# Norm sums taken beside the output products, first products begun behind each tile, values with high and low part in one stationary tile

## What is computed

```
for l in range(DEPTH):
    sh1, sc1, ga1, sh2, sc2, ga2 = split(silu(c) @ w_mod[l] + b_mod[l])      # one set for latents, one for context
    u = rmsnorm(h, g_pre_mix[l]) * (1 + sc1) + sh1
    y = token_mixers(u)         # four branches of 8 heads, gates, w_branch, w_out
    h = h + ga1 * rmsnorm(y, g_post_mix[l])
    u = rmsnorm(h, g_pre_ffn[l]) * (1 + sc2) + sh2
    a, b = split(u @ w_ffn_in[l])
    h = h + ga2 * rmsnorm((silu(a) * b) @ w_ffn_out[l], g_post_ffn[l])
```

## Time and profile before

| | |
|---|---|
| median of 3 runs | 2121.2 us (2120.85 to 2124.73) |
| the profiled execution's time | 2117.97 us |
| its span | 2116.2 us |
| TensorE busy | 1899.1 us, 90% of the span |
| VectorE, ScalarE, GpSimd busy | 1182.9, 865.7, 644.3 us |
| mean granted TensorE clock | 0.938 |

### The profile page before, as it was taken

The page is one execution under the profiler, slowest core; times in us unless marked ns, Lnnn a source line. Parts: engine busy times, 40 slices in busy tenths (PEclk is TensorE's granted clock), DMA queues, the critical chain, the costliest instruction groups (busy, mean ns, idle before and its releaser), DMA issues. The chain is left out here.

```text
span 2116.2 us, 32133 instructions
## 1 busy us (share of the span) xinstructions
PE 1899.1 (90%) x10899; PEld 1637.3 (77%) x10899; DVE 1182.9 (56%) x2360; ACT 865.7 (41%) x1870; POOL 644.3 (30%) x611
## 2 busy tenths in 40 slices
PE   8778899999988899968999999869999999979998
PEld 7566677777777777756777888757788888879997
DVE  6246666666556645268777522346564446645653
ACT  2245444444433443331222232246555545444453
POOL 6333343445444443020000100134435544311100
PEclk9989999999999999968999999779999999979998
DMA  7112333333332223215566433112344433435663
GB/s 280 53 49 60 82 85 96 95 90 108 88 84 65 70 57 122 72 60 154 174 187 193 128 95 97 45 37 64 81 120 101 115 81 91 115 95 164 183 183 109
DMA packets 391788, 223.69 MB, mean 106 GB/s; under 512 B 53398, under 2 KB 387532, under 8 KB 390604
## 3 DMA queue, kind: packets, MB, share of 16 engines
q1 hardware_dynamic: 389324, 218.50, 36.6%
q10 hardware_dynamic: 2304, 3.15, 0.5%
HBM read 218.44 MB, written 3.15 MB: 105 GB/s over the span
## 5 line engine op out<-in xcount | busy, mean ns | idle before, releaser
L1605 PE MATMUL bank<-Uhi,w_ring 128*128 128x512 f32 (+2 forms) x1664 | 604.7, 363 | 42.7 <-issue 27.1
L1606 PE MATMUL bank<-Ulo,w_ring 128*128 128x512 f32 (+2 forms) x1664 | 588.5, 354 | 0.0
L1607 PE MATMUL bank<-Uhi,w_ring 128*128 128x512 f32 (+2 forms) x1664 | 588.0, 353 | 0.0
L1361 DVE TENSOR_TENSOR w_ring<-load_ring,w_ring 128x512 fp32r<-128x512 f32 (+1 forms) x432 | 301.4, 722 | 260.1 <-ACT w_ring L1194 244.8
L1194 ACT ACTIVATE w_ring<-load_ring 128x512 fp32r<-128x512 f32 (+3 forms) x640 | 369.1, 603 | 85.2 <-PE bank L1607 74.6
L1605 PEld LDWEIGHTS bank<-Uhi,w_ring 128*128 128x128 f32 (+1 forms) x1664 | 327.1, 197 | 90.1 <-issue 32.3
L1154 POOL TENSOR_TENSOR w_ring<-load_ring,w_ring 128x512 fp32r<-128x512 f32 (+2 forms) x208 | 249.1, 1201 | 375.4 <-ACT w_ring L1194 237.7
L1607 PEld LDWEIGHTS bank<-Uhi,w_ring 128*128 128x128 f32 (+1 forms) x1664 | 326.3, 196 | 42.6
L1606 PEld LDWEIGHTS bank<-Ulo,w_ring 128*128 128x128 f32 (+1 forms) x1664 | 327.6, 197 | 36.6
L1605 PE MATMUL bank<-Z,w_ring 128*128 128x512 f32 (+2 forms) x784 | 275.6, 352 | 11.8 <-DVE Z L1500 6.1
L1606 PE MATMUL bank<-Z,w_ring 128*128 128x512 f32 (+2 forms) x784 | 269.5, 344 | 0.0
(11 more groups left out here) (114 smaller groups left out, 2414.0 us busy)
## 6 DMA issues: line engine op xcount, KB each, us to landing
load_ring<-in_w_in SPq DMA_DIRECT2D x204, 256.0 KB, 3.0
load_ring<-in_w_ffn_in SPq DMA_DIRECT2D x176, 256.0 KB, 3.2
Y<-in_w_mod SPq DMA_DIRECT2D x96, 256.0 KB, 2.8
load_ring<-in_w_ffn_out SPq DMA_DIRECT2D x80, 256.0 KB, 3.1
mod_place<-in_w_mod SPq DMA_DIRECT2D x64, 256.0 KB, 2.8
load_ring<-in_w_branch SPq DMA_DIRECT2D x64, 256.0 KB, 2.9
mod_w<-in_w_mod SPq DMA_DIRECT2D x8, 1024.0 KB, 13.8
load_ring<-in_w_in SPq DMA_DIRECT2D x64, 128.0 KB, 2.6
```

The source lines that it names most:

```text
L1361: dve.tensor_tensor(w_ring[:, slot, 1, 0:sz], load_ring[:, plan.slot['load', key], 0:sz], w_ring[:, slot, 0, 0:sz].bitcast(F32), ALU.subtr ...
L1605: pe.matmul(dst, lhs[0], rhs[0], start=start, stop=False)
L1606: pe.matmul(dst, lhs[0], rhs[1], start=False, stop=False)
L1607: return pe.matmul(dst, lhs[1], rhs[0], start=False, stop=stop)
```

## The change

1. **Sums beside the outputs.** `yev` evacuates y already multiplied by its gate coefficient (one instruction per side). Instead of `sq` and `sqmm` three quantities are made for each tile: y squared (`ysq`, ScalarE from PSUM), z squared (`zsq`, ScalarE, z the scaled y), H times z (`hz`, VectorE). GpSimd adds tiles 1 to 6 into three sums (`yadd`, `zadd`, `hadd`). At the end step `sums` has TensorE reduce the three sums and the three last tiles, 24 one-column products at 512 tokens.
2. **Turnover.** The next norm's sum is worked out from these: sum(h^2) + 2 r sum(h z) + r^2 sum(z^2) (`moment`, five small VectorE operations, and a power on GpSimd, `pow`). `bccopy` copies the first broadcast from PSUM to SBUF. `post` works in place on Y, tiles 2, 5 and 7 on GpSimd, the others on VectorE, and is interleaved with `apply`.
3. **Products behind each tile.** The first four projections (ckv, cq 0, cq 1, kr; or fa and fb of f = 0 and 1) form a group with four accumulators: `gmm` kt does their twelve products for one kt as soon as `ap_lo` of that kt is there, with weights loaded as one row piece of 416 or 512 columns. Their evacuations and the latents' norms follow behind the whole group.
4. **Values.** V is stored with high and low part side by side, 128 columns per head. `pv` takes two passes per key tile instead of three. `ov` becomes: ScalarE copies the lower half of the result to SBUF (`o_raw`), VectorE adds the upper half, ScalarE writes the high part, VectorE the low part.
5. **Modulation and splits.** In layer 1's modulation a `modw` costs its number of sides and a `modsum` 0.5, the rate is 3.7, and f = 0 and 1 have no calls. Low parts of layer 0's fa and fb pieces go to GpSimd. The coefficients of the next layer are formed ahead of w_ffn_out.

```diff
+MOD_RATE_FFN = 3.7
+POST_POOL = (2, 5, 7)
...
-        while self.todo and self.todo[0][1][0] == self.layer and self.owed >= 1:
+        while self.todo and self.todo[0][1][0] == self.layer:
             kind, key, j = self.todo[0]
+            l, ch = key
+            sides = 2 if l == 0 or ch < 16 else 1
+            cost = 1 if l == 0 else sides if kind == 'modw' else 0.5
+            if self.owed < cost:
+                break
...
+    def apply(nm, l, which, n, first, posts=None):
...
         for kt in range(KT + 1):
             if kt < KT:
                 p.take('tmp', ('ap', nm, kt), ('ap_hi', (nm, kt)), ('ap_full', (nm, kt)))
                 p.take('fil', ('ap', nm, kt), ('ap_lo', (nm, kt)))
                 p.step('apA', (nm, kt), l=l, which=which, n=n)
+                for step in posts.get(kt, ()):
+                    step()
             if kt:
                 p.step('apB', (nm, kt - 1), n=n)
+                p.step('gmm', (first, kt - 1))
...
+    def turnover(nmo, nm, l, which, n, first):
...
+        p.step('sums', nmo, n=n, what=('ysq', 'hz', 'zsq'))
+        p.step('mstat', nmo, nh=1, dim=D, n=n, after=('sums_done', nmo))
+        p.step('wide', nmo, n=n, of=1)
+        p.take('bc', ('bc', nmo), ('bc_copied', nmo))
+        p.step('bcast', nmo, n=n)
+        p.step('bccopy', nmo, n=n)
+        p.step('moment', nm, n=n)
+        p.step('pow', nm, n=n)
+        post(nmo, 0, n)
+        post(nmo, 2, n)
+        p.step('wide', nm, n=n, of=4)
+        p.take('bc', ('bc', nm), ('ap_scaled', (nm, KT - 1)))
+        p.step('bcast', nm, n=n)
+        later = {0: (1,), 1: (3, 5), 2: (4,), 3: (6, 7)}
+        apply(nm, l, which, n, first, {i: [(lambda kt=kt: post(nmo, kt, n)) for kt in kts] for i, kts in later.items()})
...
-        if key[0][0] not in ('gate', 'up', 'y', 'fa', 'fb') or key[0][0] == 'gate' and key[0][1][0] == 0:
+        what = key[0][0]
+        if what not in ('gate', 'up', 'y', 'fa', 'fb', 'first') or what in ('gate', 'fa', 'fb') and key[0][1][0] == 0 \
+                or what == 'first' and key[1] % 2:
             p.on_pool.add(key)
...
                 elif kind == 'ov':
                     act.wait_ge(sem['pv_done'], count['pv_done', key])
+                    if count['o_part', key] > 1:
+                        act.wait_ge(sem['o_lo'], count['o_lo', key] - 1)
+                    act.activation(o_raw[0:DH, :], pv_bank[DH:P, 0:SEQ], ACT.Copy).then_inc(sem['o_part'], 1)
+                    act.wait_ge(sem['o_sum'], count['o_sum', key])
...
                 elif kind == 'ov':
+                    dve.wait_ge(sem['o_part'], count['o_part', key])
+                    dve.tensor_tensor(o_raw[0:DH, :], pv_bank[0:DH, 0:SEQ], o_raw[0:DH, :],
+                                      ALU.add).then_inc(sem['o_sum'], 1)
                     dve.wait_ge(sem['o_hi'], count['o_hi', key])
...
                     for i, kt in enumerate(tiles):
-                        ins = three(pv_bank[0:DH, 0:SEQ], [a[:, kt, :] for a in v],
-                                    [pt(key, a)[:, i, :] for a in range(2)], i == 0, i == len(tiles) - 1)
+                        for a in range(2):
+                            ins = pe.matmul(pv_bank[:, 0:SEQ], v[:, kt, 2 * c0:2 * c0 + P], pt(key, a)[:, i, :],
+                                            start=i == 0 and a == 0, stop=i == len(tiles) - 1 and a == 1)
```

More of the change, by code:

```diff
@@ L138, in some @@
             self.todo.pop(0)
-            self.owed -= 1
+            self.owed -= cost
             first = False
-            l, ch = key
-            sides = 2 if l == 0 or ch < 16 else 1
             if kind == 'modw':
@@ L225, in square_sum, with group @@
         p.step('sqmm', (nm, kt), n=n)
-    def apply(nm, l, which, n):
+    def group(key, members, pieces, kt_need):
+        p.tile[key] = dict(pieces=pieces, members=members, need=kt_need)
+        for k, ring, frees, c0, cols, n in members:
+            p.take(ring, k, *frees)
+            p.tile[k] = dict(group=key, ring=ring, rows=cols, n=n)
+    def apply(nm, l, which, n, first, posts=None):
+        posts = posts or {}
         for kt in range(KT + 1):
@@ L271, in build_plan @@
         nq = SEQ if last else NTOK
[L272 to L275 removed]
+        ckv, kr, cq = (l, 'ckv'), (l, 'kr'), [(l, 'cq', 0), (l, 'cq', 1)]
+        nm, first = (l, 'pre_mix'), ('first', l, 'mix')
+        group(first, [(ckv, 'acc', [('rawsq_ready', ckv)], QL, P, NTOK), (cq[0], 'acc', [('rawsq_ready', cq[0])], 0, P, nq),
+                      (cq[1], 'spare', [('rawsq_ready', cq[1])], P, P, nq),
+                      (kr, 'merge', [('raw_ready', kr)], OFF['a_kr'] - NOPE, DA, NTOK)],
+              [dict(w='w_in', l=l, row=kt, nk=1, cols=OFF['b_q'], starts=[0]) for kt in range(KT)],
+              {kt: [('ap_lo', (nm, kt))] for kt in range(KT)})
+        if l == 0:
+            p.step('mstat', nm, nh=1, dim=D, n=NTOK, after=('sq_summed', (nm, KT - 1)))
+            p.step('wide', nm, n=NTOK, of=1)
+            p.take('bc', ('bc', nm), ('ap_scaled', (nm, KT - 1)))
+            p.step('bcast', nm, n=NTOK)
+            apply(nm, 0, 0, NTOK, first)
+        else:
+            turnover((l - 1, 'post_ffn'), nm, l, 0, NTOK, first)
         def proj(name, key, n, c0=0, cols=P, halves=None, frees=(), need=None):
@@ new lines, in output @@
+                for what in whats if 0 < dt < KT - 1 else ():
+                    p.step(what[0] + 'add', key, n=nq)
+        nmo = (l, 'post_mix')
+        output(nmo, l, 0, lambda dt: [dict(w='w_out', l=l, row=4 * j, nk=4, cols=P, starts=[dt * P]) for j in range(2)],
+               'M', lambda j: range(4 * j, 4 * j + 4), {j: [('m_lo', (l, 4 * j + 3))] for j in range(2)})
+        nm2, first = (l, 'pre_ffn'), ('first', l, 'ffn')
+        ks = [(l, f) for f in range(2)]
+        group(first, [(('fa', ks[0]), 'acc', [('ffn_silu', ks[0])], 0, P, nq), (('fa', ks[1]), 'acc', [('ffn_silu', ks[1])], P, P, nq),
+                      (('fb', ks[0]), 'spare', [('ffn_h', ks[0])], 2 * P, P, nq),
+                      (('fb', ks[1]), 'merge', [('ffn_h', ks[1])], 3 * P, P, nq)],
+              [dict(w='w_ffn_in', l=l, row=kt, nk=1, cols=4 * P, starts=[0, DFF]) for kt in range(KT)],
+              {kt: [('ap_lo', (nm2, kt))] for kt in range(KT)})
@@ L699, in build_plan, with sigmoid, hidden @@
+        turnover(nmo, nm2, l, 1, nq, first)
+        if not last:
+            mods.enter(1, ('post', 'h_new', (nmo, 4)))
+        def sigmoid(k):
+            p.take('tmp', ('ffn', k), ('ffn_h', k))
+            p.step('fsig', k, n=nq)
+        def hidden(k):
+            p.take('fil', ('ffn', k), ('hid_lo', k))
+            p.step('fh', k, n=nq)
+        for f in range(2, FT):
             k = (l, f)
@@ L708, in build_plan @@
                             [('ffn_h', k)]))
-            p.take('fil', ('ffn', k), ('hid_lo', k))
-            p.step('fh', k, n=nq)
-            mods.some(3)
+            hidden(k)
+            mods.some(MOD_RATE_FFN)
         if not last:
             mods.rest(l + 1)
+            for g in range(3):
+                p.step('coef', (l + 1, g))
         nmf = (l, 'post_ffn')
-        output('w_ffn_out', nmf,
+        output(nmf, l, 1,
                lambda dt: [dict(w='w_ffn_out', l=l, row=4 * j, nk=min(4, FT - 4 * j), cols=P, starts=[dt * P])
@@ L718, in build_plan @@
                'hid', lambda j: range(4 * j, min(4 * j + 4, FT)),
-               {j: [('hid_lo', (l, min(4 * j + 3, FT - 1)))] for j in range(-(-FT // 4))})
-        norm_stat(nmf, None, 1, D, nq, [('post_scaled', (nmf, KT - 1))])
-        if not last:
-            for g in range(3):
-                p.step('coef', (l + 1, g))
-        post(nmf, l, 1, nq, (l + 1, 'pre_mix') if not last else None)
+               {j: [('hid_lo', (l, min(4 * j + 3, FT - 1)))] for j in range(-(-FT // 4))}, ends=last)
+    p.step('sums', nmf, n=SEQ, what=('ysq',))
+    p.step('mstat', nmf, nh=1, dim=D, n=SEQ, after=('sums_done', nmf))
+    p.step('wide', nmf, n=SEQ, of=1)
+    p.take('bc', ('bc', nmf), ('bc_copied', nmf))
+    p.step('bcast', nmf, n=SEQ)
+    p.step('bccopy', nmf, n=SEQ)
+    for kt in (0, 2, 1, 3, 5, 4, 7, 6):
+        post(nmf, kt, SEQ)
     for tt in range(SEQ // P):
@@ L743, in build_plan @@
                 done += 1
-            first += st[0] == 'mm'
+            first += st[0] != 'mstat'
         order.append(st)
@@ L856, in build, with bc_bank @@
         ident = const('ident')
+        def bc_bank(nm):
+            return bank[3 + plan.slot['bc', ('bc', nm)]] if ('bc', ('bc', nm)) in plan.slot else acc(('bc', nm))
         def acc(key):
+            if ('spare', key) in plan.slot:
+                return bank[5]
             return bank[6] if ('merge', key) in plan.slot else bank[plan.slot['acc', key]]
```

317 lines of the change are left out of this document (208 added, 109 removed).

## The result

The changed kernel takes 2146.35 us (median; 2143.2 to 2149.4), the kernel before 2122.97 us in the same session: a ratio of 1.011, 95% interval 1.009 to 1.013. It is slower by 1.1%, where 2025 us was forecast; 2146 lies outside the range. The profiled execution has a span of 2141.1 us, 24.9 more than before, and a mean granted clock of 0.926.

What follows compares the result with a forecast made beforehand. TensorE was taken to bound the kernel, except at turnovers (a VectorE, GpSimd, ScalarE chain) and in the first FFN (modulation weights). Terms 17.5 + 30.8 - 2.5 + 15 + 6 + 10.5 + 2 + 15, less 1.5, gave 93: 2025 us, range 1980 to 2072.

Steps and rivals of the forecast that it cites:

- The mixer turnover with f = 0 and 1: Layer 0's mixer turnover and the first two FFN steps: ending at 932.5 instead of 963.3, gain 30.8 us, bounds 20 to 36.
- T + 21: Layer 0's turnovers: first product 21 us after T; in the mixer's, T is the last y product, and before it was T + 34.3.
- The turnover between the layers: From layer 0's FFN to layer 1: first product at T + 21, group end T + 42, gain 15 us, bounds 5 to 20.
- closing sums: Layer 0's mixer turnover: 24 one-column products, 48 records, half at 0.112 and half mostly at 0.213 us, ending at T + 7.6.
- signs named for being wrong: Splits on GpSimd near 2 us, gaps in B and C after transposes, low clock mid-FFN, or closing sums well over 8 us.
- needed two products later, so hidden: First FFN: splits of fa, fb and fh take GpSimd 3.9 of 5.5 us per half, claimed to cost no time.
- twenty f: First FFN after f = 0 and 1: 261 us against 258.5, loss 2.5; bounds gain 27 to loss 45.
- 8 us of new waits: Attention, values in two passes: 23 us of the 32.6 saved realised, less 8 of waits from the longer output chain; gain 15.
- "slower" rival: Output chain: if all 96 head outputs pay 1.2 us on TensorE, 115 us lost, total 2122 us; chance 0.05.
- port rival: First FFN: GpSimd's splits and VectorE's modulation block each other, 2.4 us per busy half, 45 in all, total 2070; chance 0.12.
- In B and C it hardly does: Attention items B and C: TensorE hardly waits for the queries' low half at unit ends, out of 29.5 us in all.
- Layer 1's mixer turnover: Half as wide: first product at T + 12 against T + 20.9, no wait for kt 7; gain 10.5 us, bounds 5 to 14.

Runs made afterwards that it cites:

- three-pass version: The changed kernel with part 4 undone (values in three passes, two-step output step): 2114.25 us, ratio 0.997.
- reordered version: Changed kernel with FFN splits on VectorE, four slots for layer 1's modulation weights, and the output step's high and low parts queued later: 2031.31 us, 0.9589.
- short output step: The changed kernel with two passes but the old two-step output step, the values' low part left out of the sum: 2083.53 us, 0.9823.

## Why the prediction was wrong

**Right, with their sizes.** The mixer turnover with f = 0 and 1 (30.3 of 30.8 us): eight serial posts and squares are gone, and the first product stands at T + 21.8 for T + 21. The turnover between the layers has its first product at T + 22. y tiles of layer 0's mixer take 5.44 us for the 5.5 taken; a values' pass takes 0.120 us, as read from the earlier trace rows (the prediction names for it). The bare norms of the latents cost about what was taken: 21.4 us before A's first query product in layer 0 for 20.4, which put it at 112.0 for 109.2, and 16.9 between the layers for 15.8.

Some luck is in the first of these. The closing sums ran at full clock in the changed kernel's trace and ended at T + 5.6 for the 7.6 taken. In seven of the later versions' traces the first product came at T + 23.9 to 24.6; in that of the three-pass version, where it came at T + 24.6, the sums took until T + 8.5. Either way the turnover is shorter by 10 us or more.

Of the signs named for being wrong, a low clock in the middle of the FFN came, and more gaps in B and C of layer 0 (TensorE idle for 14.5 and 21.9 us, 9.5 and 15.2 before). Splits on GpSimd near 2 us did not: they took 1.33.

**Wrong: "needed two products later, so hidden".** This is the step on the splits of fa and fb. The splits were indeed in time. But beside GpSimd's splits VectorE's modulation operations last 1.32 us instead of 0.48, 38% more on the average of all, and the sums of the modulation, which wait for them, stand in TensorE's queue between the FFN's products. The step asked only when the split itself is needed. The prediction had the mechanism, with the 0.97 us of the earlier trace rows, as its rival at 45 us, and gave it a chance of 0.12. Measured: 42.1 us (splits back on VectorE; 38.6 by the ratios) and 38 us (splits alone in the kernel before). The remainder of the +56.0 is a mis-sized term: with the splits on VectorE the twenty f still take 273.2 us (299.0 - 25.8) for the 261 worked out, since the first two halves after f = 0 and 1 take 12.5 and 10.1 us and halves with four pieces about 8 instead of 7.5.

**Wrong: "8 us of new waits".** The saving was undersized (30.7 for 23) and the chain by far: 52 to 63 us for the 8 taken. The bound had it (115 for 96 outputs), and the "slower" rival named it, deciding from 1.16 us a head on (by its own terms 110.6 / 96 = 1.15); but it needed less, since the port rival's 42 us came on top. The prediction reasoned that VectorE's time before that step is free, 128.8 us of waits. The waits were there; what counts is what stands behind the waiting instruction, and what stands ahead of it when the other engine is ready. Each passage from one engine to the other now stops a whole queue, ScalarE's for 0.69 us and VectorE's for 0.48 on average, and in ScalarE's are the next turned probabilities, a DMA's issue and the weights' high parts. The reordered version shows this for the larger part of the price: the same operations, 38.6 us less.

"In B and C it hardly does" was read from a kernel with the short chain. In the changed kernel layer 0's B takes 169.5 us instead of 161.2, and the clock that stood at full speed throughout it is at its lower level for 20.5 us of it. This makes the loss larger than the waits alone: TensorE's idle time there grew by 5.0 us, the stage by 8.3, although its products had become fewer.

**The range** took both rivals as apart, with one at most. Both came, and each alone would have left the time inside it or just outside: 2025 + 42 = 2067, 2025 + 49 = 2074. The smaller terms missed by some 15 us in all, each the same way.

**Mis-sized, small.** Layer 1's mixer turnover came to T + 17.5 for T + 12 taken. It takes 15.6 to 16.3 us in the versions that do not have the two passes and the blocking chain together, so 1 to 2 of the 5.5 us hang on these. TensorE's idle time in it is 9.8 us, as before (9.9); what shrank is its own work. The turnover between the layers had its second half mis-sized: the group of first products ended at T + 46 for T + 42. The end gained 0.1 for 2, which wasn't looked into. Why layer 1's mixer output gained only 0.3 of the 3.2 us in the changed kernel was not settled; the reordered version has 48.3 us there for 50.9 before, so it seems to hang on how the last items end.

**Open.** Why the chain costs 52 us beside three passes and 63 beside two wasn't taken apart, nor the 17 us by which layer 0's attention stays longer in the reordered version than with the short output step. Only the splits as a whole were moved; which of them, if any, could stay on GpSimd was not tried.

## What to carry to other kernels

Price a handover by the queue that stands still behind it, not by the duration of the two operations: an operation cut in two engines' turns should have other work put between the turns. Before work is moved to an idle GpSimd, look which VectorE operations with two SBUF operands run at that time and who waits for them, even if the moved work itself is never late. And when two losses in the bounds come from separate mechanisms, ask what the sum is if both occur.
